# Fetching only the chosen expert rows with indirect DMAs, in place of streaming the whole expert table through TensorE

## The reference

```python
q = (xn @ wq).reshape(b, s, PEER_HEADS, 2, PEER_HALF)            # 8 heads, halves of 128
sc = einsum('bshjc,hjkc->bshjk', q, subkeys)                     # 128 keys per half
top_s, top_i = lax.top_k(sc, 16)
cand = (top_s[..., 0, :, None] + top_s[..., 1, None, :])         # 256 sums
best, ci = lax.top_k(cand, 16)
idx = i1 * 128 + i2                                              # expert, from ci and top_i
g = softmax(best)
act = gelu(einsum('ckd,cd->ck', u_tab[idx], x))                  # 128 experts per position
y = einsum('ck,ckd->cd', g * act, v_tab[idx])                    # sum of their down rows
```

## Time and profile before

| | |
|---|---|
| median of 3 executions | 2727.94 us (2727.94, 2724.69, 3168.57) |
| span of the profiled execution, first to last instruction | 2725.5 us |
| PE busy | 2501.0 us, 92% of the span |
| DVE busy | 1856.3 us, 68% |
| ACT busy | 1072.0 us, 39% |
| POOL busy | 667.9 us, 25% |
| mean granted TensorE clock | 0.944 of full |
| DMA | 392.39 MB, mean 144 GB/s |

### The profile page before, as it was taken

The page is one execution under the profiler, slowest core; times in us unless marked ns, Lnnn a source line. Parts: engine busy times, 40 slices in busy tenths (PEclk is TensorE's granted clock), DMA queues, the critical chain, the costliest instruction groups (busy, mean ns, idle before and its releaser), DMA issues. The chain is left out here.

```text
span 2725.5 us, 43333 instructions
## 1 busy us (share of the span) xinstructions
PE 2501.0 (92%) x15400; PEld 2241.7 (82%) x15400; DVE 1856.3 (68%) x3364; ACT 1072.0 (39%) x1798; POOL 667.9 (25%) x628
## 2 busy tenths in 40 slices
PE   7879989999999999888798899999999997687898
PEld 7747877999999999786687789999999996687897
DVE  7585897666666666596678976666666666559552
ACT  4321544444444444433225444444444444434321
POOL 4592572000000000066716700000000003336240
PEclk9869999999999999897799999999999998888898
DMA  5424304555555555443342055555555553233101
GB/s 203 141 95 160 124 1 133 188 188 185 185 186 188 188 186 188 142 161 133 136 135 78 3 192 187 188 187 185 185 185 188 188 186 116 89 137 132 47 1 39
DMA packets 107672, 392.39 MB, mean 144 GB/s; under 512 B 11952, under 2 KB 13360, under 8 KB 107184
## 3 DMA queue, kind: packets, MB, share of 16 engines
q1 hardware_dynamic: 107568, 391.02, 42.7%
HBM read 389.93 MB, written 1.05 MB: 143 GB/s over the span
## 5 line engine op out<-in xcount | busy, mean ns | idle before, releaser
L621 PE MATMUL bank<-chunk_parts,weight_parts 128*128 128x512 f32 x3072 | 747.0, 393 | 7.2 <-DVE chunk_parts L1238 7.2
L609 PEld LDWEIGHTS bank<-x_parts,chunk_parts 128*128 128x128 f32 x5760 | 722.6, 192 | 18.5
L609 PE MATMUL bank<-x_parts,chunk_parts 128*128 128x256 f32 x5760 | 728.3, 283 | 0.0
L1238 DVE TENSOR_TENSOR chunk_parts<-weight_ring,chunk_parts 128x1024 fp32r<-128x1024 f32 x496 | 606.0, 1222 | 179.1 <-ACT chunk_parts L841 179.1
L841 ACT CAST chunk_parts<-weight_ring 128x1024 fp32r<-128x1024 f32 x496 | 518.8, 1046 | 363.6 <-PE bank L621 363.6
L621 PEld LDWEIGHTS bank<-chunk_parts,weight_parts 128*128 128x128 f32 x3072 | 563.4, 189 | 117.8 <-DVE chunk_parts L1238 9.7
L1230 DVE TENSOR_TENSOR work<-work,big 128x256 f32<-128x256 f32 x256 | 163.1, 637 | 275.8 <-ACT work L845 260.9
L845 ACT ACTIVATE work<-bank 128x256 f32<-128x256 f32 x240 | 92.1, 384 | 440.0 <-PE bank L609 440.0
L885 POOL MEMSET big<- 128x572 f32 x2 | 1.1, 574 | 719.8 <-issue 713.7
L1531 PE MATMUL bank<-x_parts,chunk_parts 128*128 128x256 f32 x1152 | 151.7, 296 | 26.0 <-POOL chunk_parts L1521 26.0
L1437 POOL MEMSET big<- 128x24 f32 x1 | 0.1, 123 | 713.5 <-issue 713.5
(11 more groups left out here) (373 smaller groups left out, 2992.7 us busy)
## 6 DMA issues: line engine op xcount, KB each, us to landing
weight_ring<-in_experts SPq DMA_DIRECT2D x512, 512.0 KB, 3.3
big<-in_ada SPq DMA_DIRECT2D x48, 512.0 KB, 3.9
weight_ring<-in_w_in SPq DMA_DIRECT2D x40, 512.0 KB, 4.4
weight_ring<-in_wq SPq DMA_DIRECT2D x32, 512.0 KB, 3.4
weight_ring<-in_gdn_in SPq DMA_DIRECT2D x32, 512.0 KB, 3.3
weight_ring<-in_w_out SPq DMA_DIRECT2D x16, 640.0 KB, 3.9
weight_ring<-in_lru_in SPq DMA_DIRECT2D x16, 512.0 KB, 3.3
weight_ring<-in_w_kv SPq DMA_DIRECT2D x8, 512.0 KB, 4.3
```

The lines of the kernel that those rows point to most:

```text
L609: last = nc.tensor.matmul(nc_ps[2 + n % 2][:, 0:T], a[:, j * P:(j + 1) * P], xr[:, x, j], start=(j == 0 and a is hi and x == 0), stop=(j = ...
L621: last = nc.tensor.matmul(nc_ps[4 + 2 * tt + c][:, 0:512], wr[:, x, n % 2, tt * P:(tt + 1) * P], v[:, c * 512:(c + 1) * 512], start=False, ...
L1238: nc.vector.tensor_tensor(split[:, k % SPLITS, 1], wring[:, (N_RING + k) % WSLOTS, 0:D], split[:, k % SPLITS, 0].bitcast(F32), ALU.subtrac ...
```

## The change

The unit of work becomes one fetch: for v = 0 to 255 it stands for a half of the positions (128 of them, one on each partition), a head and one of its 16 places. One indirect DMA, issued by POOL, reads for each partition the row of the expert that its position chose, 128 rows of 8 KB (up and down row side by side in a table laid out anew), 1 MB in all. It lands in one of 11 buffers. DVE multiplies the up half with the position's vector x, which lies in PSUM, and sums it (`dot`). ACT applies gelu, multiplies by the gate and scales the identity by the result (`weight`). PE multiplies this diagonal matrix with the down half in two plain-f32 matmuls of 128x512 and accumulates (`down`). The gate matrix, the early up tiles, the dense stream and the split in two parts for PEER are gone. Scores of three heads and the expert numbers of two are made ahead of the first `dot`; query tiles, scores, ranking and gates of the others are written in between the units. The loop over the two layers is unrolled, and the decoding of indices moves from POOL to DVE.

```diff
-NE = 2 * NK
-N_EARLY = 8
+NEXPERT = NK * NK
+UNITS = NT * SLOTS
+ROW = 2 * D
+NBUF = 11
+NDIAG = 4
+EARLY_HEADS = 3
+TILES_AT = {3 + 4 * i: EARLY_HEADS + i for i in range(PH - EARLY_HEADS)}
+SCORES_AT = {at + 1: h for at, h in TILES_AT.items()}
+CHOICE_AT = {TOPK * i + 7: EARLY_HEADS + i for i in range(PH - EARLY_HEADS + 1)}
+EXP_AT = {at + 2: a - 1 for at, a in CHOICE_AT.items()}
+GATES_AT = {at + 8: a - 1 for at, a in CHOICE_AT.items()}
+TURN_X_AT = 28
+KEEP_FIRST_AT = SLOTS + 3
+TURN_FIRST_AT = SLOTS + 5
+ADD_FIRST_AT = SLOTS + 8
+    x_rows = [ps_all[:, at:at + D] for at in (4 * 512, 2 * 512)]
+    sums_e = [ps_all[:, at:at + D] for at in (6 * 512, 0)]
+    def unit(v):
+        return v // SLOTS, v % SLOTS // TOPK, v % TOPK
-    with nc.Fori(0, LAYERS) as l:
+    for l in range(LAYERS):
             (SP)
-                with sp.Fori(0, NSTREAM // WSLOTS - 1) as i:
-                    for e in range(WSLOTS):
-                        sp.wait_ge(s("lo_done"), i * WSLOTS + (e + 1))
-                        sp.dma_start(wring[:, (N_RING + e) % WSLOTS, 0:D], d_e[l, i * WSLOTS + (N_EARLY + e + WSLOTS)]).then_inc(...)
             (TensorE)
-                (early_up, gate matrix, up and down of the dense stream)
+                def down(v):
+                    tt = unit(v)[0]
+                    pe.wait_ge(s("diag_ready"), v + 1)
+                    for c in range(2):
+                        last = nc.tensor.matmul(sums_e[tt][:, c * 512:(c + 1) * 512], diag[:, v % NDIAG],
+                                                rows_e[v % NBUF][:, D + c * 512:D + (c + 1) * 512],
+                                                start=(v % SLOTS == 0), stop=(v % SLOTS == SLOTS - 1))
+                    last.then_inc(s("down_done"), 1)
+                query_tile(0)
+                query_tile(1)
+                pe.wait_ge(s("out_added"), KD)
+                turn_x(0)
+                pe.wait_ge(s("sub_loaded"), 32)
+                key_scores(0)
+                for h in range(1, EARLY_HEADS):
+                    query_tile(2 * h)
+                    query_tile(2 * h + 1)
+                    key_scores(h)
+                for v in range(UNITS):
+                    down(v)
+                    if v in TILES_AT:
+                        query_tile(2 * TILES_AT[v])
+                        query_tile(2 * TILES_AT[v] + 1)
+                    if v in SCORES_AT:
+                        key_scores(SCORES_AT[v])
+                    ...
+                turn_out(1)
             (ScalarE)
+                def weight(v):
+                    tt, h, a = unit(v)
+                    act.wait_ge(s("dot_done"), v + 1)
+                    nc.scalar.activation(acts[:, v:v + 1], dots[:, v:v + 1], ACT.Gelu).then_inc(s("act_done"), 1)
+                    if v % TOPK == 0 and tt == 0:
+                        act.wait_ge(s("gates_ready"), h + 1)
+                    act.wait_ge(s("act_done"), v + 1)
+                    nc.scalar.activation(gated[:, v:v + 1], acts[:, v:v + 1], ACT.Copy, scale=gate[:, h, tt, a:a + 1]).then_inc(s("gated"), 1)
+                    if v >= NDIAG:
+                        act.wait_ge(s("down_done"), v - NDIAG + 1)
+                    act.wait_ge(s("gated"), v + 1)
+                    nc.scalar.activation(diag[:, v % NDIAG], ident, ACT.Copy, scale=gated[:, v:v + 1]).then_inc(s("diag_ready"), 1)
             (GpSimd)
-                (candidates, keyed, and the products with the gates)
+                for v in range(UNITS):
+                    tt, h, a = unit(v)
+                    if v % TOPK == 0 and tt == 0:
+                        pool.wait_ge(s("experts_ready"), h + 1)
+                    if v >= NBUF:
+                        pool.wait_ge(s("down_done"), v - NBUF + 1)
+                    nc.gpsimd.indirect_dma_start(rows_e[v % NBUF], None, d_e, bass.IndirectOffsetOnAxis(ap=expert[:, h, tt, a:a + 1], axis=0)
+                                                 ).then_inc(arrived(f"rows_loaded{v % NBUF}"), 16)
             (VectorE)
+                def dot(v):
+                    ...
+                    dve.wait_ge(arrived(f"rows_loaded{v % NBUF}"), 16 * (l * loads(v % NBUF) + v // NBUF + 1))
+                    nc.vector.scalar_tensor_tensor(waste[:, v % 2], rows_e[v % NBUF][:, 0:D], 1.0, x_rows[tt], ALU.mult, ALU.mult,
+                                                   accum_out=dots[:, v:v + 1]).then_inc(s("dot_done"), 1)
+                choose(0, None)
+                choose(None, 0)
+                decode(0)
+                choose(1, None)
+                choose(2, 1)
+                decode(1)
+                gates(0)
+                gates(1)
+                for v in range(UNITS):
+                    dot(v)
+                    if v in CHOICE_AT:
+                        a = CHOICE_AT[v]
+                        choose(a if a < PH else None, a - 1)
+                        decode(a - 1)
+                    if v in GATES_AT:
+                        gates(GATES_AT[v])
+                    if v == ADD_FIRST_AT:
+                        out_add(0)
+                out_add(1)
+    a["experts"] = np.concatenate([f["peer_u"].reshape(L * NEXPERT, D), f["peer_v"].reshape(L * NEXPERT, D)], axis=1)
-    nc = bacc.Bacc(..., dynamic_dma_scratch_size=1024)
+    nc = bacc.Bacc(..., dynamic_dma_scratch_size=4096)
```

More of the change, by code:

```diff
@@ L549, in _ @@
                             pe.wait_ge(s("ffn_ready"), k + 1)
[L550 removed]
+                        last = nc.tensor.matmul(query_bank(m), wt[:, k], xn[:, k], start=(k == 0), stop=(k == KD - 1))
                     last.then_inc(s("w_used"), 1)
[L552 to L556 removed]
@@ L557, in early_up @@
-                def early_up(n):
-                    wt = w_tile(N_ALL + n)[:, 0:D].rearrange("p (k c) -> p k c", k=KD)
-                    if n < HBANKS:
-                        pe.wait_ge(s("query_kept"), 2 * PH)
-                    else:
-                        pe.wait_ge(s("early_kept"), n - HBANKS + 1)
-                    for k in range(KD):
-                        last = nc.tensor.matmul(nc_ps[n % HBANKS][:, 0:T], wt[:, k], xn[:, k], start=(k == 0), stop=(k == KD - 1))
-                    last.then_inc(s("w_used"), 1)
@@ L583, in _ @@
-                for g in range(GROUPS):
-                    pe.wait_ge(s("first_gated"), g + 1)
-                    pe.wait_ge(s("second_hot"), g + 1)
-                    if g == 0:
-                        pe.wait_ge(s("slots_kept"), 1)
-                    if g >= G_BANKS:
-                        pe.wait_ge(s("g_kept"), g - G_BANKS + 1)
-                    for j in range(4):
-                        last = nc.tensor.matmul(nc_ps[g % G_BANKS][:, j * P:(j + 1) * P], ha[:, g % HOTS, j], hb[:, g % HOTS, j], start=True, stop=True)
-                    last.then_inc(s("g_ready"), 1)
@@ L613, in down @@
-                def down(n, k, ready, wgt_, stop=False):
-                    pe.wait_ge(s("lo_done"), ready)
-                    pe.wait_ge(s("wgt_ready"), wgt_)
-                    hi, lo = split[:, k % SPLITS, 0], split[:, k % SPLITS, 1]
-                    for tt in range(NT):
-                        for x, v in ((0, hi), (0, lo), (1, hi)):
-                            for c in range(2):
-                                last = nc.tensor.matmul(nc_ps[4 + 2 * tt + c][:, 0:512], wr[:, x, n % 2, tt * P:(tt + 1) * P],
-                                                        v[:, c * 512:(c + 1) * 512], start=False, stop=stop and x == 1, skip_group_check=True)
-                    last.then_inc(s("split_used"), 1)
@@ L821, in _ @@
-                act.wait_ge(s("best_shifted"), 1)
-                nc.scalar.activation(ex, ex, ACT.Exp).then_inc(s("best_exp"), 1)
-                index_float(PH - 1)
-                for n in range(6, N_EARLY):
-                    early_keep(n)
-                for j in range(2):
-                    act.wait_ge(s("slots_turned"), j + 1)
-                    if j == 0:
-                        nc.scalar.copy(slot[:, 2], nc_ps[2][:, 0:T])
-                    last = nc.scalar.copy(slot[:, j], nc_ps[j][:, 0:T])
@@ L877, in _, with out_keep @@
+                def out_keep(tt):
+                    act.wait_ge(s("down_done"), (tt + 1) * SLOTS)
                     for c in range(2):
-                        last = nc.scalar.copy(out_e[:, c * 512:(c + 1) * 512], nc_ps[4 + 2 * tt + c][:, :])
+                        last = nc.scalar.copy(out_e[tt][:, c * 512:(c + 1) * 512], sums_e[tt][:, c * 512:(c + 1) * 512])
                     last.then_inc(s("peer_kept"), 1)
+                for h in range(EARLY_HEADS):
+                    query_keep(2 * h)
+                    query_keep(2 * h + 1)
+                    score_keep(h)
@@ new lines, in _ @@
+                for h in range(EARLY_HEADS - 1):
+                    best_exp(h)
+                for v in range(UNITS):
+                    weight(v)
+                    if v in TILES_AT:
+                        query_keep(2 * TILES_AT[v])
```

(7 more changed lines are left out.)

486 lines of the change are left out of this document (126 added, 360 removed).

## The result

The changed kernel takes **2380.48 us** (median of 4 runs, 2378.23 to 2382.64), the kernel before 2727.11 in the same comparison: a ratio of 0.873, 95% interval 0.872 to 0.874. The profiled execution is the fastest of the four, 2378.23 us, with a span of 2376.4 us; the median lies 4.1 us above that span.

A forecast was written before the change was run, and what follows sets the result against it. The prediction held the old dense stage bound by PE and the new stream by DMA. Per layer 30 + 256 R + 119 - 31 R + 9 = 158 + 225 R, 765.5 us against 896.6, gave 2728 - 262 = 2466 us; forecast's range 2385 to 2600.

The forecast's parts named there:

- R: Expert stream in each PEER part: time per unit, that of the slowest engine, DMA, at 2.7 us; lower end 2.54.
- outside the PEER parts: Everything but the two PEER parts: keeps its code and its 932.3 us; unrolling the layer loop costed at nothing.
- Lead: Start of each PEER part: first indirect DMA 27 us in, 30 us with the wait for first data.
- Tail: End of each PEER part, from the last `dot` through copies, transposes and addition: 9 us.
- Stall in the start: Early units of each part: stream waits for PE, busy with late query tiles, to free buffers; 119 - 31 R, 35 us.
- Choices hidden by eleven buffers: After the start: six choices of 15 us on DVE; 16 dots and a choice take 35 us against 43 of stream.
- PE: Each unit's `down`: four records of 512 columns, 1.82 us, leaving PE 0.9 us idle per unit.
- `dot`: Each unit's DVE multiply and sum of 1024 elements, one operand in PSUM: 1.2 to 1.4 us.
- POOL's issue: One indirect DMA per unit: 1.5 us, between 0.33 and 2.44, hidden by the 2.7 us of DMA.
- Rival B: Gather runs at the queue's mean pace, 336 GB/s, 3.12 us per unit: 2655 us; chance 0.19.
- Rival C: POOL's indirect issue, held up by DVE's `dot`, becomes the bound at 3.66 us per unit: 2898 us; chance 0.18.
- Rival D: PE, pausing in every unit, runs at half clock, 3.64 us per unit: 3115 us; chance 0.05.

The follow-up runs named there:

- Experiments 1 to 3: Changed kernel with 128 neighbouring rows per unit, with two gathers of 4 KB rows, and with plain 2 KB pieces: 2378.24, 2413.26 and 2480.12 us.
- Experiment 8: Changed kernel with five heads' query tiles and scores ahead of the stream, the other three spread out: 2309.19 us.
- Experiments 5 and 6: Changed kernel with six, then four row buffers in place of eleven: 2465.1 and 2740.08 us.
- experiment 4: Changed kernel with both operands of `dot` in SBUF and ten buffers: 2387.52 us, against 2383.92 for the changed kernel with ten buffers.

## Why the prediction missed

The working follows the prediction's own steps. **The step that failed is R and its lower bound.** I took 2.7 us from the 392 GB/s of an 8 us stretch and 2.54 as the end, from 413 GB/s over 4 us. The 4 us were of 4 KB rows; of the 8 us a third of the bytes came in 8 KB rows (128 packets of 716), but the queue was not full all through (share 0.98). The unit now has 8 KB rows in a queue eleven deep and takes 2.488 us. Experiments 1 to 3 show the two parts of the error: 4 KB rows in as full a queue would have been 2.564 (which is 0.136 of the 0.212 us), and 8 KB rows give the remaining 0.076. With 225 units that count per layer, (2.7 - 2.488) x 225 x 2 = **95 us**. The bound was no bound: I read the best 4 us of another piece size as the most that the queue can do. A line in pieces was the way to a lower end, and the trace of before has no full stretch of 8 KB rows to draw it from, so nothing gave me the right to end the range at 413 GB/s. Of the prediction's own estimates of R, the 2.47 us that it set aside in favour of rows 7 came nearest.

The whole account from 2466: R -95.4; outside the PEER parts 922.5 in place of 932.3, -9.8; each part about 9.1 us longer than 158 + 225 x 2.488 = 717.8, +18.3 for both; the median above the span by 4.1 in place of 2.4, +1.7. That is 2380.8; measured 2380.5. With the right R alone the sum would have given 2370, so the other terms were off too, by 18.3 us one way and 9.8 the other, and it is luck that they nearly cancel.

- **Lead:** first issue 25.4 us after the part's start, 27 expected. Right. Tail: 7.9 us, 9 expected. Right.
- **Stall in the start:** 119 - 31 x 2.488 = 42 expected. The part less a lead of 28.4, 256 units and a tail of 7.9 leaves 53. The mechanism was the named one: POOL waits of 9.3 to 10.4 us for `down` at 310, 329, 351, 370 and 388 us, five as counted, about 19.5 us apart in place of 18.6. In addition the weights of the late tiles pass through the same DMA engines (queue q1, 3.17 MB from 270 to 960 us, 7.5 us at 421 GB/s). I had left them out. Experiment 8, which removes the stall and gains 71 us, shows that the stall came from where the tiles stood; that "a faster stream only waits longer here" was not tried apart.

```profile
299.81 0.94 POOL L832 DMA_INDIRECT big<-in_experts,big  x1 [0.78 <-PE banks L570]
310.08 0.94 POOL L832 DMA_INDIRECT big<-in_experts,big  x1 [9.34 <-PE banks L570]
...
329.28 0.94 POOL L832 DMA_INDIRECT big<-in_experts,big  x1 [10.35 <-PE banks L570]
```

- **Choices hidden by eleven buffers:** right; 421 GB/s with and without them. Experiments 5 and 6 show it from the other side.
- **PE** was priced at 1.82 us; it needs 1.72 to 1.73. **`dot`** 1.22 + 0.08, inside 1.2 to 1.4. **ACT** about 1.0: 0.20, 0.29 and 0.40 us with gaps, right. **POOL's issue** 0.94, where I took 1.5 between 0.33 and 2.44: right in that it is hidden.
- **Rival B** (336 GB/s) did not come: the program's mean contained transfers with nothing behind them, as the argument against it said, and it is what four buffers bring about. **Rival C** did not: with two SBUF operands DVE does hold the issues up, at a tenth of the price, and with one in PSUM hardly at all (experiment 4). The page "SBUF — State Buffer" (section "SBUF: two separate sides") of the Trainium skill, which spoke for C, says that a DVE operation with two SBUF inputs and a GpSimd operation that reads SBUF exclude each other; those 89 stretched issues agree with it in direction. **Rival D** did not in the steady part: the clock was full from 560 to 900 us with PE busy for 271.8 of 340 us. Half clock did come in two other places, each time after a pause of PE: for the first four downs (0.50 from 286 to 295 us, PE idle for 21.3 us before 289.7), and after choices between 400 and 560 us (0.87 in the mean; PE idle for 9.5 us before 433.5 and before 473.3). The queue stayed full there all the same:

```profile
430.00:440.00 10.00, 6.46 (x10) 2.79 (x11) 9.97 (x17) 6.74 (x18) 0.97 (x2) 0.57 1.01 421
```

Together B, C and D had 0.42 of the chance, and they pulled the range up; its low end was left to the one bound that was wrong.

## What to carry to other kernels

When a change makes a DMA queue the bound, price the unit by its bytes *and* its pieces, and do not take the best short stretch of smaller pieces for the most that the queue can give: here 2 KB, 4 KB and 8 KB pieces gave 387, 409 and 421 GB/s. A gather of twice the bytes won because it starts 25 us into the part, where the dense stage stood behind 213 us of choices and gate matrix (242.7 to 456 us); and from 400 us on it kept its rate because eleven buffers outlast every stop there. Count the buffers against the longest stop (six and four cost 85 and 360 us). After that, look at what the in-order engines meet in the first buffers' worth of units: query tiles put there cost 71 us, and put right ahead of their reader they cost 95.

## What the runs showed of the hardware

- An indirect DMA of 128 rows costs POOL 0.94 us whether the rows are 4 or 8 KB (and is 1.24 us from one to the next), a plain one of 128 rows 0.53, one of 512 pieces 0.75.
- Scattered 8 KB rows are read as fast as neighbouring ones, 421 GB/s on one core.
- Each piece of 2 to 8 KB costs about 9.5 ns on its DMA engine beside its bytes (a line through 2.488, 2.564 and 2.710 us per unit).
- With both operands of `dot` in SBUF, 89 of 512 indirect issues on POOL took over 1.1 us, at most 1.99; with one in PSUM 4 or 5 of 512 (the control, the changed kernel).
